# A decoder step on one core: the index projection merged into one product of 584 columns, x transposed through a scaled identity, and the small tables loaded as rows

## The chip, the cores and the metric

The kernel runs on one core of a Trainium2 chip. The metric is the device time of one execution in microseconds (us); the time of a kernel is the median of its runs. All data are float32 unless a line says otherwise.

## What is computed

One inference step of a one-layer decoder for a prompt of 512 tokens and eight samples of eight tokens (64 rows), 576 tokens of width 1024 in all. The part that the change touches:

```
def project_mixer_inputs(xn, w_in, pos):            # xn = rms_norm(x, attn_norm_g)
    q, k, v, qi, ki, wi, u, ga, gb = jnp.split(xn @ w_in, cuts, axis=-1)
    q = rope(...); k = rope(...); qi = rope(...)     # qi: 8 index heads of 64
    ki = rope(ki)                                    # one index key of 64 per token
def indexer_select(qi, wi, ki_all, q_pos, n_sel):    # wi: 8 weights per token
    s = einsum('bqhd,bld->bqhl', qi, ki_all) * IDX_DIM ** -0.5
    score = einsum('bqhl,bqh->bql', relu(s), wi * N_IDX_HEADS ** -0.5)
    _, idx = lax.top_k(where(admissible, score, -inf), n_sel)
```

After it come attention over the selected keys (the samples read keys, values and index keys from a paged cache through `page_table`), a pooling branch, two gates, an output product with a residual, a mixture of 32 experts with two chosen per token, and a last norm. The columns of `w_in` for qi, ki and wi lie side by side: 512, 64 and 8 of them, from column 1024.

## The kernel before

It is written engine by engine, each with its own order of instructions, tied together by semaphores. There is no scheduler: the order in the text is the order on the engine. Tokens go in five tiles (`TILES`): four of 128 prompt tokens and one of 64 sample rows. Everything lives in one SBUF tensor `arena`, cut up by hand, and in the eight banks of `psum`.

The front of the program, around which the change is made, runs so:

- **Loads.** SyncE's queue issues the identity and a column `lane` (L418), the five tiles of x (L420), the page table as eight broadcast loads of single columns (L424), the two norm gains and the pooling scale, turned on the way so that each partition gets single elements (L425 to L427), the 72 columns for ki and wi (`kiww`, L428), the 512 columns for qi (ring slot 0, L442), the rest of the constants with the rotary tables (L445), the history and the pooling weights (L446, L447), the columns for q (L442). L452 then writes zeros into 8 MB of `y_d`, once GpSimd has cleared `zrow`. A "ring" of two slots holds the blocks of 512 columns, and `load_ring(n)` waits until the products of block n-2 are done (`RING_USED`).
- **Norm and transposition.** For each tile ScalarE sums the squares (L1085), takes the root (L1088) and later writes x times 1/rms into `xs` (`scale_x`, L1076), after VectorE's reciprocal (L1340). TensorE transposes `xs` in eight blocks (L613), VectorE multiplies by the gain on the way out of PSUM into `xnT` (L1354). VectorE waits for all three gain loads (`gain_in`, 48) in front of its first L1354, and its third reciprocal stands behind that wait.
- **First products.** `first_product(i)` makes ki and wi of tile i (72 columns, L590), and ScalarE takes them (L1096, L1097). Then come the qi products of tiles 1 to 4 (`QI_ORDER`, 512 columns, L590); tile 0 needs none, since its tokens see fewer keys than are selected. GpSimd gathers the index keys of the samples from the cache (L1662), then rotates ki of each tile (`rotate`, L1693 to L1704) and stores it (L1716), and rotates the jobs of the list `JOBS` (qi, q, k), each after ScalarE's copy out of PSUM (`take_raw`, L1113).
- **Index scores.** `turn_keys` (L633 to L639) and `turn` (L625) transpose the rotated keys and queries, `turned` (L1067) copies them out. `index_prompt(j)` multiplies them (L652), ScalarE applies relu (L1134) and VectorE adds up the eight heads with their weights (L1367 for the first, L1370 for seven more), for j = 0, 1, 2 over 256, 384 and 512 keys. TensorE makes the product of tile i+2 or of q between them.
- **Selection.** VectorE then makes the weights of the samples (L1372) and selects, by rounds of eight (L1383, L1385), for three prompt tiles and for the samples; the last mask is written at L1406. Beside it TensorE scores the samples (L676 to L698), then makes q, k, u (L590, L587), the pooling branch (L728 to L740) and six parts of the gates (L756). Attention starts with L772, and its second unit needs VectorE (L1436) behind the masks.

## Time and profile before

| | us |
|---|---|
| median of 3 runs | 1123.46 |
| lowest and highest | 1121.77, 1126.6 |
| the profiled execution | 1127.28 |
| its span | 1125.7 |
| TensorE busy | 945.2 (84%) |
| VectorE busy | 337.1 (30%) |
| ScalarE, GpSimd busy | 207.3, 201.1 (18% each) |

Time inside the profile counts from the start of the span. Matmuls appear as PE, weight loads as PEld. A float32 product of one block shows as two MATMUL instructions, a transposition as one. "SPq" is SyncE's queue, and an issue there is not the transfer: the transfer lands later.

### The profile page before, as it was taken

Reading aid. Unit: us, or ns where it says so; the run is one execution under the profiler, and the core shown is the slowest. Engines: PE = TensorE matmul, PEld = TensorE weight load, DVE = VectorE, ACT = ScalarE, POOL = GpSimd, SP = SyncE. Lnnn points to the kernel's source line nnn. Section 1 sums busy time; section 2 is a strip of 40 time slices with the busy share of each in tenths; the row PEclk is TensorE's granted clock in tenths of the full one; section 3 lists DMA queues with packets and bytes.
Section 4 is the critical chain, followed back from the end, with each engine's and each line's share of the span. In section 5 each row is a group of like instructions: output and inputs, shape, how many; then the busy total and the mean of one; then the engine's idle time right before and its main releaser. Section 6 shows DMA issues by size and latency. Waiting matters only on the chain.

```text
span 1125.7 us, 11532 instructions
## 1 busy us (share of the span) xinstructions
PE 945.2 (84%) x4386; PEld 506.7 (45%) x4386; DVE 337.1 (30%) x736; ACT 207.3 (18%) x450; POOL 201.1 (18%) x312
## 2 busy tenths in 40 slices
PE   3997999989999998989994998878778887878860
PEld 3643444667776656764552433333233332332320
DVE  1059999993341110331225001000000000000006
ACT  4144111212334334000221100000000000000012
POOL 2750452100001110000132111111111111011113
PEclk9998999999999999999996999999999999998995
DMA  6950022332202645943025999999999999999947
GB/s 210 391 195 1 5 99 91 109 122 75 76 1 75 223 152 159 334 158 150 19 92 213 387 406 425 426 423 424 423 423 424 426 424 423 424 424 425 416 165 245
DMA packets 56414, 283.72 MB, mean 252 GB/s; under 512 B 13224, under 2 KB 13944, under 8 KB 37423
## 3 DMA queue, kind: packets, MB, share of 16 engines
q1 hardware_dynamic: 45591, 246.23, 54.7%
q0 software_dynamic: 10784, 36.97, 9.0%
q8 instruction: 25, 0.41, 0.1%
q14 instruction: 14, 0.11, 0.0%
HBM read 267.38 MB, written 23.17 MB: 258 GB/s over the span
## 4 chain that ended last, share of the span: by engine, by line
PE 64%; DVE 18%; issue 7%; ACT 4%; DMA 4%; SPq 3%; POOL 0%; POOLq 0%; ACTq 0%; DVEq 0%
PE psum L994 21%; PE psum L1009 10%; PE psum L756 8%; DVE arena L1385 6%; DVE arena L1383 6%; PE psum L910 5%; PE psum L590 4%; PE psum L892 3%; DMA arena<-in_w_branch_pool 2%; PE psum L1002 1%; PE psum L844 1%; DVE arena L1611 1%; ACT arena L1283 1%; ACT arena L1287 1%; PE psum L810 1%
## 5 line engine op out<-in xcount | busy, mean ns | idle before, releaser
L994 PE MATMUL psum<-arena 128*64 128x512 f32 x992 | 236.9, 632 | 55.9 <-issue 55.1
L994 PEld LDWEIGHTS psum<-arena 128*64 128x64 f32 x992 | 85.8, 145 | 205.5 <-issue 205.5
L1009 PE MATMUL psum<-arena 128*64 128x512 f32 x512 | 116.9, 597 | 17.7 <-ACT arena L1287 17.7
L756 PE MATMUL psum<-arena 128*128 128x288 f32 x480 | 126.0, 415 | 0.0
L590 PE MATMUL psum<-arena 128*128 128x512 f32 (+2 forms) x320 | 120.2, 535 | 2.1 <-ACT arena L1152 2.1
L756 PEld LDWEIGHTS psum<-arena 128*128 128x128 f32 x480 | 89.6, 192 | 30.9 <-issue 8.1
L1611 DVE TENSOR_TENSOR arena<-arena,psum 128x256 f32<-128x256 f32 x32 | 13.5, 421 | 289.6 <-ACT arena L1283 289.6
L1283 ACT ACTIVATE arena<-psum 128x256 f32<-128x256 f32 x32 | 12.3, 383 | 415.8 <-PE psum L994 405.0
L590 PEld LDWEIGHTS psum<-arena 128*128 128x128 f32 (+1 forms) x320 | 57.6, 207 | 55.0 <-issue 52.4
L1009 PEld LDWEIGHTS psum<-arena 128*64 128x64 f32 x512 | 40.5, 136 | 72.1 <-issue 72.1
L892 PE MATMUL psum<-arena 128*128 128x288 f32 x256 | 64.3, 415 | 5.9 <-DMA arena<-in_w_branch_pool 5.9
L1615 DVE COPY arena<-psum 128x512 f32<-128x512 f32 x32 | 22.1, 691 | 157.1 <-PE psum L1009 157.1
L1383 DVE MAX8 arena<-arena 64x8 f32<-64x1032 f32 (+3 forms) x80 | 66.2, 828 | 2.8
L1797 POOL CAST arena<-arena 128x1 int32 x30 | 5.5, 183 | 329.1 <-DVE arena L1615 329.1
L1385 DVE MATCH_REPLACE8 arena<-arena 64x1032 f32<-64x1032 f32 (+3 forms) x76 | 61.8, 814 | 0.0
L1067 ACT COPY arena<-psum 128x512 f32<-128x512 f32 (+6 forms) x104 | 46.9, 495 | 67.3 <-PE psum L783 32.0
L892 PEld LDWEIGHTS psum<-arena 128*128 128x128 f32 x256 | 49.6, 194 | 20.6 <-DMA arena<-in_w_branch_pool 6.8
L910 PE MATMUL psum<-arena 128*128 128x512 f32 x128 | 55.8, 593 | 1.1 <-issue 1.1
L1665 POOL DMA_INDIRECT arena<-xn_d,arena x32 | 33.4, 1043 | 34.2 <-POOL arena L1791 25.9
L1669 POOL DMA_INDIRECT y_d<-arena x32 | 33.1, 1034 | 29.0 <-POOL arena L1797 27.4
L910 PEld LDWEIGHTS psum<-arena 128*128 128x128 f32 x128 | 23.9, 190 | 29.7 <-issue 29.7
L1773 POOL TENSOR_TENSOR arena<-arena 128x1024 f32<-128x1024 f32 (+1 forms) x5 | 11.7, 2350 | 141.2 <-ACT arena L1271 141.2
(249 smaller groups left out, 882.8 us busy)
## 6 DMA issues: line engine op xcount, KB each, us to landing
arena<-in_w_exp_down SPq DMA_DIRECT2D x32, 2048.0 KB, 22.9
arena<-in_w_exp_gate SPq DMA_DIRECT2D x31, 2048.0 KB, 17.8
arena<-in_w_exp_up SPq DMA_DIRECT2D x30, 2048.0 KB, 22.3
arena<-in_w_in SPq DMA_DIRECT2D x8, 2048.0 KB, 8.7
y_d<-arena SPq DMA_DIRECT2D x1, 8192.0 KB
arena<-in_x_prompt SPq DMA_DIRECT2D x8, 512.0 KB, 7.5
arena<-in_w_out SPq DMA_DIRECT2D x2, 2048.0 KB, 10.7
arena<-in_w_exp_up SPq DMA_DIRECT2D x4, 1024.0 KB, 12.9
```

The costliest lines, as they stand in the source:

```text
L590: last = pe.matmul(bank(b, n, slice(0, r)), lhs, w[:, k, 0:n], start=(k == 0), stop=(k == KD - 1))
L756: last = pe.matmul(bank(2 + n % 2 if n < SAMPLE_G else 2, HN), ring[slot % 2][:, k, m * P:(m + 1) * P], xnT[:, k, HN * hh:HN * hh + HN], s ...
L892: last = pe.matmul(bank(b, HN), w[:, 4 * br + k, m * P:(m + 1) * P], src[:, k, tc], start=(k == 0), stop=(k == 3))
L910: last = pe.matmul(bank(4 + 2 * (i % 2) + half), sgA[k][:, i * P:(i + 1) * P], ring[half][:, k, :], start=(k == 0), stop=(k == KD - 1))
L994: last = pe.matmul(bank(2 + s, 512, rows).rearrange("p (w n) -> p w n", w=2), x_k, wgu[s][:, :, DE * k + 256 * q:DE * k + 256 * q + 256], ...
L1009: last = pe.matmul(bank(4 + s, 512, slice(64 * half, 64 * half + 64)), hT[s][:, k % 2, CAP * (k // 2):CAP * (k // 2) + CAP], wd[s][:, k, 5 ...
L1067: last = act.copy(out, src(b))
L1383: link(dve.max(m8, src))
L1385: link(dve.match_replace(w, m8, src, LOW))
L1611: dve.tensor_tensor(hb[s], sg[s], bank(2 + s, DE // 2, at0=DE // 2), ALU.mult).then_inc(m["h_ready"], 1)
L1665: pool.indirect_dma_start(xg[s], None, xn2_d, bass.IndirectOffsetOnAxis(ap=sidx[s], axis=0), bounds_check=2 * NT - 1, oob_is_err=False).th ...
L1669: pool.indirect_dma_start(y_halves, bass.IndirectOffsetOnAxis(ap=syid[s], axis=0), yo[s], None, bounds_check=2 * FIRST - 1, oob_is_err=Fal ...
```

## The change

Five things are edited together.

1. **One product.** The 584 columns of qi, ki and wi are loaded as one block `wqi` (a place of its own, in front of the ring), and `qi_product` makes them for tiles 1 to 4 in two halves of 292 columns. Tile 0 gets ki alone, 64 columns. The 72-column block, `first_product` and the first ring load are gone, and the ring starts with q.
2. **x through a scaled identity.** ScalarE no longer scales x. VectorE multiplies the identity by 1/rms (`scaled_ident`, 128 by 128), and TensorE multiplies x by that in place of the transposition (`turn_x`). All four prompt tiles are turned first; the sample tile follows after the product of tile 1.
3. **Small loads as rows.** The gains come as 20 rows of 128 and the page table as 8 rows of 8, issued from ScalarE's queue, and TensorE transposes them. VectorE widens the page table in between.
4. **GpSimd's order.** The gathers go in two fours in front of jobs 0 and 1, the key of a tile is rotated with its query as a ninth head, and the keys are transposed in parts (0 and 1, 2, 3, then the samples).
5. **Constants and zeros.** The rotary tables are loaded ahead of the rest, `zrow` moves to the end of the arena, and nothing holds back its clearing. ScalarE's wait for `fill_out` in the pooling branch is gone.

TensorE, from the start to the first index scores. L613 are transpositions of x, L590 products; in the changed kernel L616 turns x, L628 is the key of tile 0 and L604 the product in halves. Before:

```order
L613 MATMUL psum<-arena 128x128 x16
L590 MATMUL psum<-arena 128x72 x8
L613 MATMUL psum<-arena 128x128 x8
L590 MATMUL psum<-arena 128x72 x8
...
L590 MATMUL psum<-arena 64x72 x8
L590 MATMUL psum<-arena 128x512 x14
L633 MATMUL psum<-arena 128x128 x4
...
L590 MATMUL psum<-arena 128x512 x8
L625 MATMUL psum<-arena 128x128 x4
L590 MATMUL psum<-arena 128x512 x2
L652 MATMUL psum<-arena 128x256 x8
```

The same place in the changed kernel (L621 and L623 transpose the gains and the page table, L649 keys, L641 the query, L663 are the scores):

```order
L621 MATMUL psum<-arena 128x20
L623 MATMUL psum<-arena 128x8
L616 MATMUL psum<-arena 128x128 x32
L628 MATMUL psum<-arena 128x64 x8
L604 MATMUL psum<-arena 128x292 x16
L616 MATMUL psum<-arena 128x64 x8
L604 MATMUL psum<-arena 128x292 x32
L649 MATMUL psum<-arena 128x128 x2
L641 MATMUL psum<-arena 128x128 x4
L663 MATMUL psum<-arena 128x256 x8
L604 MATMUL psum<-arena 64x292 x16
```

The four full-width products, which stood between the transpositions and the first scores as 24 blocks of 512, are three products of 16 halves now, and the product of the sample tile has moved behind the first scores.

GpSimd, from its first row of work to its second index query. L1662 and L1698 are the gathers, L1704 and L1737 the sums of a key, L1716 and L1742 its store. Before:

```order
L1662 DMA arena<-in_cache_idx_k,arena 128x512 x8
L1675 MEMSET arena 128x512
...
L1704 TENSOR_TENSOR arena<-arena 64x64 x2
L1716 DMA out<-arena 64x64
L1693 TENSOR_TENSOR arena<-arena 128x8x32 x2
```

And in the changed kernel:

```order
L1708 MEMSET arena 128x512
...
L1742 DMA out<-arena 128x64
L1698 DMA arena<-in_cache_idx_k,arena 128x512 x4
L1726 TENSOR_TENSOR arena<-arena 128x9x32 x2
L1727 TENSOR_TENSOR arena<-arena 128x9x32
L1728 TENSOR_TENSOR arena<-arena 128x9x32
L1737 TENSOR_TENSOR arena<-arena 128x64 x2
L1779 TENSOR_TENSOR arena<-arena 128x512
L1742 DMA out<-arena 128x64
L1698 DMA arena<-in_cache_idx_k,arena 128x512 x4
```

The clearing of `zrow` now comes first, and eight gathers and five keys no longer stand ahead of the queries: four gathers and one key do.

The diff, cut to what the sections above name:

```diff
-        RING_LOADS = [w_in_v[:, :, c:c + 512] for c in (C_QI, C_Q, C_K, C_U)]
+        RING_LOADS = [w_in_v[:, :, c:c + 512] for c in (C_Q, C_K, C_U)]
-        RING_USED = [(S["jp"], v) for v in (9, 14, 19, 24)] + [(S["g_done"], v) for v in (8, 16, 24, 32, 48, 64)]
+        RING_USED = [(S["jp"], v) for v in (10, 15, 20)] + [(S["g_done"], v) for v in (8, 16, 24, 32, 48, 64)]
...
-                for j in range(NPAGE):
-                    src = page_table[:, j:j + 1].rearrange("b j -> j b").to_broadcast([GR, DB])
-                    sp.dma_start(pgi[GR * j:GR * (j + 1), :], src).then_inc(S["page_in"], 16)
-                sp.dma_start(gain1, attn_norm_g[0].rearrange("(k p) -> p k", p=P)).then_inc(S["gain_in"], 16)
...
-                sp.dma_start(kiww, w_in_v[:, :, C_KI:C_KI + KIW]).then_inc(S["kiww_in"], 16)
+            sp.dma_start(wqi, w_in_v[:, :, C_QI:C_QI + QIW]).then_inc(S["wqi_in"], 16)
+            c1 = where["bandcur"][0]
+            sp.dma_start(arena[:, c0:c1], consts[:, c0:c1]).then_inc(S["tab_in"], 16)
...
+            def qi_product(i):
+                r = rows_of(i)
+                pe.wait_ge(S["xn_ready"], 2 * (i + 1))
+                b = QI_BANK[i]
+                for k in range(KD):
+                    lhs = xnT[:, k, i * P:i * P + r]
+                    for half in range(2):
+                        out = bank(b, QIH, slice(64 * half, 64 * half + 64)) if r == 64 else bank(b + half, QIH)
+                        last = pe.matmul(out, lhs, wqi[:, k, QIH * half:QIH * half + QIH], start=(k == 0), stop=(k == KD - 1))
+                last.then_inc(S["jp"], 1)
+
+            def turn_x(i):
...
+                pe.wait_ge(S["dg_ready"], i + 1)
...
-                        last = pe.transpose(bank(g % 2, r, at0=k * P), xs[i % 2][0:r, kk * P:(kk + 1) * P], ident[0:r, 0:r])
+                        last = pe.matmul(bank(g % 2, r, at0=k * P), xin[i][0:r, kk * P:(kk + 1) * P], diag[i % 2][0:r, 0:r], start=True, stop=True)
...
+            pe.wait_ge(S["gain_in"], 48)
+            pe.transpose(bank(2, 20), grow, ident[0:20, 0:20]).then_inc(S["gain_t"], 1)
+            pe.wait_ge(S["pg_wide"], 1)
+            pe.transpose(bank(3, DB), pgw, ident[0:DB, 0:DB]).then_inc(S["gain_t"], 1)
+            for i in range(PT_TILES):
+                turn_x(i)
+            pe.wait_ge(S["wqi_in"], 16)
+            for k in range(KD):
+                last = pe.matmul(bank(6, HD), xnT[:, k, 0:P], wqi[:, k, NI * HD:NI * HD + HD], start=(k == 0), stop=(k == KD - 1))
+            last.then_inc(S["jp"], 1)
+            qi_product(1)
+            turn_x(PT_TILES)
+            pe.wait_ge(S["je"], 1)
+            qi_product(2)
...
+            pe.wait_ge(S["je"], 2)
+            pe.wait_ge(S["xn_ready"], 2 * TILES)
+            qi_product(3)
+            turn_keys(0, 1)
+            turn(0, 4, P, P)
+            index_prompt(0)
+            pe.wait_ge(S["je"], 4)
+            qi_product(PT_TILES)
+            turn_keys(2)
+            turn(1, 4, P, P)
+            index_prompt(1)
+            ring_ready(R_Q)
+            project(0, ring[R_Q % 2], 512)
+            turn_keys(3)
+            turn(2, 4, P, P)
+            index_prompt(2)
...
-                act.activation(xs[i % 2][0:r, :], xin[i][0:r, :], ACT.Copy, scale=rstd1[0:r, i:i + 1]).then_inc(S["xs_ready"], 1)
+            for row, g in ((0, attn_norm_g), (8, ffn_norm_g), (16, pool_scale)):
+                n = g.shape[1] // P
+                act.dma_start(grow[row:row + n, :], g[0].rearrange("(k p) -> k p", p=P)).then_inc(S["gain_in"], 16)
+            act.dma_start(pgi, page_table).then_inc(S["page_in"], 16)
...
+            def take_qi(job):
...
+                act.copy(raw[job % 2][0:r, 0:QIH], lo)
+                act.copy(raw[job % 2][0:r, QIH:NI * HD + HD], hi[:, 0:QIH - NI])
+                act.activation(wiS[0:r, i, :], hi[:, QIH - NI:QIH], ACT.Copy, scale=float(HD ** -0.5 * NI ** -0.5)).then_inc(S["je"], 1)
...
+            def scaled_ident(i):
                 dve.wait_ge(S["rt_done"], i + 1)
-                dve.reciprocal(rstd1[:, i:i + 1], rt1[:, i:i + 1]).then_inc(S["rstd_ready"], 1)
-
-            inverse_rms(0)
-            inverse_rms(1)
-            dve.wait_ge(S["gain_in"], 48)
+                link(dve.reciprocal(rstd1[:, i:i + 1], rt1[:, i:i + 1]))
+                if i >= 2:
+                    dve.wait_ge(S["xt_done"], 2 * (i - 1))
+                dve.tensor_scalar(diag[i % 2], ident, rstd1[:, i:i + 1], None, ALU.mult).then_inc(S["dg_ready"], 1)
...
-            pool.wait_ge(S["gi_ready"], 1)
-            for b in range(DB):
-                gather(idxk[:, b, :], i_groups, gidx[:, b:b + 1], s_idx)
...
+                if kind == "qi" and job < 2:
+                    for b in range(4 * job, 4 * job + 4):
+                        gather(idxk[:, b, :], i_groups, gidx[:, b:b + 1], s_idx)
```

## Rows read from the trace of the kernel before

**Rows 1.** Chain of waits, 0 to 60 us: start, us, what.
```profile
11.66 7.57 DMA arena<-in_ffn_norm_g
...
35.07 15.29 PE psum L590 x60
...
58.12 0.44 PE psum L625 x4
```

**Rows 2.** Timeline, VectorE's index scores: start, busy us, engine, line, operation.
```profile
61.59 0.79 DVE L1367 TENSOR_SCALAR arena<-arena 128x256 f32<-128x256 f32 x1 [25.66 <-ACT arena L1134]
...
68.88 0.58 DVE L1367 TENSOR_SCALAR arena<-arena 128x384 f32<-128x384 f32 x1 [1.16 <-ACT arena L1134]
...
80.18 0.66 DVE L1367 TENSOR_SCALAR arena<-arena 128x512 f32<-128x512 f32 x1 [3.63 <-ACT arena L1134]
...
87.91 0.41 DVE L1372 TENSOR_TENSOR arena<-arena,psum 128x256 f32<-128x256 f32 x1
```

**Rows 3.** Timeline, where sample scoring starts and where TensorE waits for the masks.
```profile
88.42 1.94 PE L676 MATMUL psum<-arena 128*128 128x128 f32 x8 [2.19 <-issue]
...
111.52 8.83 PE L590 MATMUL psum<-arena 128*128 128x512 f32 x16 [2.10 <-ACT arena L1152]
...
244.24 4.15 PE L756 MATMUL psum<-arena 128*128 128x288 f32 x16
251.26 0.52 PE L772 MATMUL psum<-arena 64*128 64x128 f32 x4 [2.88 <-DVE arena L1436]
```

**Rows 4.** Timeline: page table issues, a gather, GpSimd's first query, copy of a turned query.
```profile
3.93 4.55 SPq L424 DMA_DIRECT2D arena<-in_page_table  x8
...
23.74 0.95 POOL L1662 DMA_INDIRECT arena<-in_cache_idx_k,arena  x1 [0.30 <-issue]
...
45.91 1.24 POOL L1693 TENSOR_TENSOR arena<-arena 128x256 f32<-128x256 f32 x2 [0.22 <-ACT arena L1113]
...
58.60 0.58 ACT L1067 COPY arena<-psum 128x512 f32<-128x512 f32 x1 [5.00 <-PE psum L625]
```

**Rows 5.** Timeline, tile 0 of x from its landing to TensorE.
```profile
5.37 1.03 ACT L1085 ACTIVATE psum<-arena 128x1024 f32<-128x1024 f32 x1 [2.89 <-DMA arena<-in_x_prompt]
...
6.55 0.29 ACT L1088 ACTIVATE arena<-arena 128x1 f32<-128x1 f32 x1
...
9.40 1.94 PE L613 MATMUL psum<-arena 128*128 128x128 f32 x8 [9.40 <-ACT arena L1076]
```

**Rows 6.** Windows: length, PE, PEld, DVE, ACT, POOL busy (count), PEclk, DMA share, GB/s.
```profile
28.00:29.00 1.00, 1.00 (x7) 1.00 (x6) 0.00 (x0) 0.53 (x3) 0.70 (x2) 1.00 0.97 407
...
36.00:38.00 2.00, 2.00 (x25) 1.93 (x24) 0.00 (x0) 0.29 (x2) 1.60 (x8) 1.00 1.12 387
...
94.00:96.00 2.00, 2.00 (x8) 1.09 (x7) 1.86 (x8) 1.38 (x3) 0.00 (x0) 0.85 0.00 0
...
113.00:115.00 2.00, 2.00 (x4) 0.67 (x3) 1.90 (x5) 0.00 (x0) 0.00 (x0) 0.50 0.00 0
```

**Rows 7.** Timeline, unit prices at the full clock: transpositions, products of 128, 288 and 2 by 256.
```profile
97.82 1.09 PE L676 MATMUL psum<-arena 128*128 128x128 f32 x8
...
205.71 0.39 PE L728 MATMUL psum<-arena 128*128 128x128 f32 x2
...
205.93 0.39 PE L729 MATMUL psum<-arena 128*128 128x128 f32 x2
...
220.39 23.50 PE L756 MATMUL psum<-arena 128*128 128x288 f32 x96
...
201.11 3.67 PE L587 MATMUL psum<-arena 128*64 128x256 f32 x32
```

**Rows 8.** DMA issues by line: KB each and median us from issue to landing.
```profile
arena<-in_w_in SPq DMA_DIRECT2D x8, 2048.0 KB, 8.7
...
arena<-in_page_table SPq DMA_DIRECT2D x8, 0.5 KB, 7.8
...
arena<-in_consts SPq DMA_DIRECT2D x1, 64.5 KB, 1.8
```

More of the change, by code:

```diff
@@ L50 @@
 KIW = HD + NI
+QIW = NI * HD + KIW
+QIH = QIW // 2
 HN = NT // 2
@@ L186, in program @@
         poT = at(POT, 4, NT)
-        zrow = at(POT, 512)
+        zrow = at(AW - 512, 512)
+        wqi = at(ATT, KD, QIW)
         ring = [at(RING + s * SLOT, KD, 512) for s in range(2)]
         stats = at(XNT - 64, 64)
+        grow = at(SMALL, P, rows=20)
         gain1 = stats[:, 0:8]
@@ L463, in _ @@
                 sp.dma_start(vnew[:, b, :], vnat[b * DS:(b + 1) * DS, PT_TILES, :]).then_inc(S["vnew_in"], 16)
-            for n in range(5, 8):
+            for n in range(4, 7):
                 load_ring(n)
@@ L909, in out_proj @@
                     for k in range(KD):
-                        last = pe.matmul(bank(4 + 2 * (i % 2) + half), sgA[k][:, i * P:(i + 1) * P], ring[half][:, k, :],
+                        last = pe.matmul(bank(4 + 2 * (i % 2) + half), sgA[k][:, i * P:(i + 1) * P], ring[(R_OUT + half) % 2][:, k, :],
                                          start=(k == 0), stop=(k == KD - 1))
@@ L1347, in _ @@
                 r = rows_of(i)
-                if half == 0 and i + 2 < TILES:
-                    inverse_rms(i + 2)
-                if g == 2:
-                    dve.wait_ge(S["page_in"], 16 * NPAGE)
-                    dve.tensor_scalar(gidx, pgi, float(GR), const("lane"), ALU.mult, ALU.add).then_inc(S["gi_ready"], 1)
                 dve.wait_ge(S["xt_done"], g + 1)
@@ L1355, in _ @@
                                   gain1[:, 4 * half:4 * half + 4].unsqueeze(2).to_broadcast([P, 4, r]), ALU.mult).then_inc(S["xn_ready"], 1)
+                if half and i + 2 < TILES:
+                    scaled_ident(i + 2)
             dve.wait_ge(S["const2_in"], 16)
@@ L1695, in rotate @@
                 link(pool.tensor_tensor(b[:, :, 1, :], x[:, :, 0, :], t("sin"), ALU.mult))
-                if outs is None:
-                    for h4 in range(2):
-                        four = slice(4 * HD * h4, 4 * HD * (h4 + 1))
-                        last = pool.tensor_tensor(roped[job % 2][:, four].rearrange("p (j g c) -> p g j c", j=2, g=2),
-                                                  rtmp[0][:, four].rearrange("p (g j c) -> p g j c", j=2, g=2),
-                                                  rtmp[1][:, four].rearrange("p (g j c) -> p g j c", j=2, g=2), ALU.add)
-                    return last
@@ new lines, in key_out, with store_key @@
+            def key_out(i, h):
+                r = rows_of(i)
+                c = slice(h * HD, h * HD + HD)
+                for d in range(2):
+                    last = pool.tensor_tensor(kir[0:r, i, HD * d:HD * d + HD], rtmp[0][0:r, c], rtmp[1][0:r, c], ALU.add)
+                last.then_inc(S["ki_roped"], 1)
+            def store_key(i):
+                pool.wait_ge(S["ki_roped"], i + 1)
+                pool.dma_start(ni_rows[i], kir[0:rows_of(i), i, 0:HD]).then_inc(S["ki_out"], 16)
```

194 lines of the change are left out of this document (94 added, 100 removed).

## The prediction

> **What bounds the kernel now.** I read the chain of waits first, for what the end hangs on. From the start it runs over SyncE's small loads: the last gain lands at 19.2 us, and VectorE, which waits for it in front of its first evacuation, lets go of everything behind [rows 1]. In the timeline tile 0 of x is in at 5.4 us and its root is done at 6.8, so some 11 us go by with the data there [rows 5]. Then the chain is TensorE without a break (transpositions, products of 72 and 512 columns) until the first index query is turned at 58.6 [rows 1]. VectorE's scores start at 61.6, 68.9 and 80.2, each pass after a wait for ScalarE and so for TensorE, and end with the weights of the samples at 88.3 [rows 2]. From there VectorE selects without a gap until 250.6. Beside it TensorE starts to score the samples when those weights are there (88.4), starts the q products at 111.5 and is through at 248.4. It then waits 2.9 us for the masks [rows 3]. So both long strands hang on one point, the end of the index scores, and they are nearly equal: what comes off the front moves both, and neither has to be shortened. What follows (attention, gates, experts) starts by semaphores of this chain and has no fixed hour. The zeros for y_d, the one big transfer with an hour of its own, are issued at 31.6 today, and earlier after the change.
>
> I forecast where the three passes start and compare the last one with 80.2.
>
> **The start.** The eight page table issues alone hold SyncE's queue for 4.6 us, and each lands 7.8 us after its issue [rows 4, 8]. They and the three gains leave this queue. As rows they have no price in this trace. Bounds: the identity, 64 KB, landed in 1.8 us, and the element-wise loads in 7.8 [rows 8]. I take 2.5, near the identity, because the new form also moves whole rows; issued from ScalarE by about 2.6 us they are in at about 5. The two little transpositions, VectorE's copy between them and the page index are then done at about 7, beside the root of tile 0, which is ready at 6.84 [rows 5]. Reciprocal and scaled identity (two short VectorE steps with handoffs, 0.8 us in all): TensorE starts at 7.6. ScalarE, without scale_x, needs some 1.4 us a tile and stays ahead. A page of the Trainium skill speaks against an early landing: "DMA: Bandwidth & Descriptors", § Issuing engines are not separate DMA queues, says that transfers of all issuing engines share the same 16 engines and interleave, so a second queue saves issue time only. By that the rows might trail the x tiles; the late-landing rival below has that price.
>
> **Turning x.** A block is a product now, two instructions for one. At the full clock a transposition of 128 takes 1.09 / 8 = 0.136 us. L728 and L729 start 0.22 apart with two instructions each, 0.112 per instruction [rows 7]. So a tile costs 16 x 0.112 = 1.8 us against 1.1. TensorE begins slow, though. Between 28 and 29 it makes 7 instructions in 1 us, though the clock column reads 1.00 there, and between 36 and 38 it makes 25 in 2 [rows 6]: until 33 to 34 it ran at the lower of its two levels, 1.2 GHz, and tile 0's eight transpositions took 1.94 us [rows 5]. When will it rise? Work that began at 111.5 was at 2.4 GHz (0.98) from about 115; work from 88.4 with a gap in it, from about 94.7 (0.85 over 94 to 96); dense work from 20.2 only from 33.5 [rows 3, 6]. So 3.5, 6.3 and 13.4 us after the start. I take 5, between the first two, because the new stream has 128 columns in every instruction, where that of 20 to 33 had 72 in most. Four tiles are 64 x 0.107 = 6.8 us at speed, plus 2.5 for five slow us: all turned at 16.9.
>
> **Waiting for the weights.** wqi is 2.39 MB and queues behind x, which is through at about 9. Loads of 2 MB land in 8.7 us [rows 8]; at the 390 GB/s or so of the full windows it needs 6.1 us and a latency, hence 16 to 17. It just hides; up to 1.5 us late is inside my range. Its copy of constants (0.25 MB) follows and GpSimd needs that at 19.
>
> **The products.** 288 columns take 23.5 / 96 = 0.245 us an instruction [rows 7], so 292 take 0.248 and a tile of 32 takes 7.9 us. The key of tile 0 is 16 weight-bound instructions, 1.8 us (to 18.7). Tile 1 is done at 26.6, the sample tile of x (16 instructions, where eight transpositions were) at 28.3, tile 2 at 36.2, tile 3 at 44.1. Before, the second query's turn ended at 58.6 and TensorE had by then made most of the same columns; the gain up to here is the idle time, the slow clock and the sample product that moved back.
>
> **First pass.** After the turn at 58.6 the first score came at 61.6 [rows 1, 2], of which 0.9 us was a leftover of the next product: 2.1. Now ScalarE stands on this path with its copy of tile 3 (three pieces, 1.1 us) and one of the keys (0.4) ahead of the 0.6 of the query [rows 4]: 44.1 + 3.6 = 47.7. Before, 61.6. Gain here 13.9.
>
> **Second pass.** The sample product now stands behind the first scores. TensorE leaves those at about 49; the product costs 3.67 x 292 / 256 = 4.2 us [rows 7]; turns 0.7; ScalarE's take 1.1, key copy 0.2, query 0.6, and 1.8 to the first relu: 56.9. VectorE is free at 53.8 (61.6 to 67.7 is its pass, 6.1) and waits 3 us. Gain 12.
>
> **Third pass.** Index products 3.4 from 55.1, tile 0 of q 7.0 (16 x 0.43 and a start), ScalarE 0.8 + 0.3 + 0.6, then 2.2 to VectorE: 69.2, where 80.2 stood. **Gain 11.0.** The extra copies and the moved product give back 3 of 14. The pass of 7.7 and the sample weights stay, so selection starts at 77 and the masks end at 239.6.
>
> **GpSimd** must keep up. Zeros and qs first, from 1 us on, nothing waits. Key 0 rotated at 21, four gathers of 1.25, job 0 from 28 to 33, a store, four gathers until 38.7, job 1 until 43.5 (needed at 53), job 2 from 45.5 to 50.2 (needed by ScalarE's next take at 53), job 3 until 61 (needed at 71). A ninth head adds 1/8 to four steps and two small ones, 0.9 us a job, hidden by TensorE's products; without that cover it would cost 0.9 at one pass. The gathers land by 50 and are needed at 77. The ring is ahead: q and k lie ready, u loads at the same point relative to its use. The zeros to y_d run until about 52 with nobody waiting. ScalarE's wait for fill_out was long met, worth nothing. I cost these at nothing.
>
> **Sum.** 11.0 off. The profiled execution took 1127.28 (span 1125.7), 0.34% over the median 1123.46; it would take 1116.3, and the median becomes **1112.5**. Own range: clock rise 3.5 to 6.3 after the start (0.7 less or more), weights up to 1.5 late, 1 us either way in ScalarE's handoffs, 2 for the scatter of runs: 1109 to 1116.
>
> **Rivals.**
> - *The clock rises late*, 13.4 us after the start as from 20.2 on [rows 6], at 21. Then 8.4 more us pass at half speed, 4.2 lost, 1116.7; in the worst such case at 33.5 as now, 10.5 lost, 1123. For it: the one precedent of the front. Against: narrower instructions there. Chance 0.14.
> - *The rows land late*, 7.8 after issue as the old small loads [rows 8], behind x: page table at 10.4, TensorE from 12.2, 4.6 lost, 1117.1. Against: the identity's 1.8. Chance 0.08.
> - *The price of turning is far higher.* Were a block four times a transposition, 0.54 us for 0.136 [rows 7], then 24 to 32 blocks of x would add about 10 us in front and 2 for the sample tile: 1124. The skill's page "TensorE: Matmul & The Clock Gate", Terms, calls the transposing mode 4 times faster for FP32; by that this case would follow. L728 shows 0.22 per product, 1.6 times, so 0.03.
> - *No gain*: the front is shorter, but a strand behind it keeps its hour, the samples' gathers or a ring load. 1123.5. Against: each lies 20 us ahead of its use. 0.03.
> - *Slower*: the front never reaches the high clock, since TensorE alternates with VectorE and ScalarE there. Its place is the products of 292 columns. At half speed turning ends at 21.3, the key at 24.9, and three products and a turn take 50.6: 75.5 in place of 44.1, and the last pass comes 35 us late: some 1147. It decides from a rise later than about 35 us (each us at 1.2 GHz costs half of one against my 12.6, and 11 are there to lose). Against: L756, 288 wide, runs at the full clock. Chance 0.04.
> - A gain above 13 (faster rise, quieter VectorE): 0.02.
>
> **Numbers.** Forecast 0.66. What a measurement of this kernel can tell from no change is about 0.5%, 5.6 us, so faster means below 1117.8: 0.66 + 0.02 + 0.10 of the clock's 0.14 + 0.05 of the late rows' 0.08 = 0.83. Same: the rest of these two, the dear turn and no gain, 0.13. Slower 0.04. The range 1108 to 1120 adds to my own the two milder rivals and leaves out some 0.2.
>
> **What would show it.** Right: first turn of x at 7 to 8 us, all prompt tiles turned by 17 with instructions at 0.11 in the second half, the three scoring passes from about 47.7, 57 and 69, selection from 77, TensorE's wait for the masks still about 3 us, and every later stage moved by the same 11. Wrong: PE instructions of x still 0.21 apart at 20; a gap ahead of the key product for wqi_in; GpSimd ending job 1 after 53; or a wait of VectorE ahead of the third pass above 5 us. If the front gains 11 and the end doesn't, the mistake is in my claim that nothing behind has an hour of its own.

## The result, and the profile after

| | before | after |
|---|---|---|
| median of seven runs each, us | 1123.48 | 1115.16 |
| ratio of the runs, 95% interval | | 0.9898 (0.9876 to 0.9919) |
| profiled execution: time, span, us | 1127.28, 1125.7 | 1115.16, 1113.5 |
| third pass of scores starts, us | 80.18 | 69.43 |
| SyncE issues the load of w_branch_attn, us | 435.16 | 423.76 |

The kernel is faster by 1.0%. The medians differ by 8.3 us; the ratio of the runs, 0.9898, stands for 11.5 us, its interval for 9 to 14. A median of 1112.5 (1108 to 1120) was forecast. In the profiled executions the span is 12.2 us shorter, of which 10.75 are there at the third pass and 11.4 at the load of w_branch_attn. That issue hangs on a semaphore of the main strand, and I use it below as a landmark behind the attention's front. One execution each of two experiments below (1646.04 us in e1_rows_only, 2289.39 us in e4_split_512_72) stands far off for a reason not known, and the ratios leave it out.

The chain of waits of the kernel after, 0 to 60 us, where [rows 1] stood (start, us, what):

```profile
2.29 4.52 DMA arena<-in_page_table
...
8.15 9.64 PE psum L616 x64
17.79 1.73 PE psum L628 x16
19.52 7.92 PE psum L604 x32
27.44 1.93 PE psum L616 x16
29.37 15.95 PE psum L604 x64
...
47.67 0.61 ACT arena L1165
```

The 7.57 us of the last gain are gone. The chain begins with the page table, now 64 numbers in rows, and from 8.15 to 45.32 it is TensorE alone: four tiles turned by scaled identities (L616), the key of tile 0 (L628), three query products (L604) with the sample tile's turn between them. VectorE's passes and the sample weights follow, in place of [rows 2] (timeline: start, busy us, engine, line, operation, idle time before):

```profile
48.31 0.71 DVE L1403 TENSOR_SCALAR arena<-arena 128x256 f32<-128x256 f32 x1 [17.68 <-ACT arena L1165]
...
57.16 0.42 DVE L1403 TENSOR_SCALAR arena<-arena 128x384 f32<-128x384 f32 x1 [2.90 <-ACT arena L1165]
...
69.43 0.70 DVE L1403 TENSOR_SCALAR arena<-arena 128x512 f32<-128x512 f32 x1 [5.01 <-ACT arena L1165]
...
76.31 0.41 DVE L1408 TENSOR_TENSOR arena<-arena,psum 128x256 f32<-128x256 f32 x1
```

The transfers of 0 to 40 us: the rate of each us in GB/s, then issues with KB each and median us to landing:

```profile
GB/s 0 3 145 256 352 399 417 422 397 175 231 348 390 399 404 392 383 383 385 385 387 393 467 436 433 433 311 219 257 307 362 380 390 377 391 393 385 402 422 416
...
arena<-in_w_in SPq DMA_DIRECT2D x1, 2336.0 KB, 13.3
...
arena<-in_x_sample SPq DMA_DIRECT2D x1, 256.0 KB, 8.3
```

At 9 to 11 us the rate falls by half, and the sample tile takes 8.3 us. The index columns, issued at 4.16, are in at about 17.5, 0.3 us ahead of their use.

TensorE's wait for the masks, as in [rows 3], kept its length, and the sixteen product instructions behind it took 5.84 us where the same sixteen ahead of it took 4.15. Timeline of TensorE, then windows of the same stretch (length, PE, PEld, DVE, ACT, POOL busy with counts, PEclk, DMA share, GB/s):

```profile
232.93 4.15 PE L780 MATMUL psum<-arena 128*128 128x288 f32 x16
239.82 0.49 PE L796 MATMUL psum<-arena 64*128 64x128 f32 x4 [2.75 <-DVE arena L1472]
240.25 5.84 PE L780 MATMUL psum<-arena 128*128 128x288 f32 x16
```

```profile
240.00:242.00 2.00, 2.00 (x8) 1.46 (x9) 1.57 (x9) 1.76 (x8) 0.00 (x0) 0.60 0.00 0
242.00:244.00 2.00, 2.00 (x6) 1.38 (x6) 0.03 (x1) 0.00 (x0) 0.00 (x0) 0.54 0.00 0
```

The granted clock is 0.60 and 0.54 there, close to the lower level of 1.2 GHz. The kernel before had the same (5.77 us behind 2.88 us idle), so it doesn't enter the comparison; it comes back below.

### The profile page after: what moved, and what is told of

Its sections match the earlier page's. It is cut to its first block, busy times and chain, and to the rows that moved or that the text cites. A ratio compares the mean times of both kernels' runs of the same rounds, so it can differ in the third digit from the quotient of the medians.

```text
span 1113.5 us, 11556 instructions
## 1 busy us (share of the span) xinstructions
PE 944.4 (85%) x4412; PEld 510.2 (46%) x4412; DVE 338.7 (30%) x743; ACT 201.7 (18%) x445; POOL 198.3 (18%) x296
## 4 chain that ended last, share of the span: by engine, by line
PE 64%; DVE 18%; issue 7%; ACT 4%; DMA 3%; SPq 2%; POOL 1%; ACTq 0%; POOLq 0%; DVEq 0%
PE psum L1018 21%; PE psum L1033 11%; PE psum L780 9%; DVE arena L1421 6%; DVE arena L1419 6%; PE psum L934 5%; PE psum L916 3%; PE psum L604 3%; DMA arena<-in_w_branch_pool 2%; PE psum L1026 1%; PE psum L868 1%; DVE arena L1647 1%; ACT arena L1313 1%; ACT arena L1317 1%; PE psum L834 1%
## 5 line engine op out<-in xcount | busy, mean ns | idle before, releaser
L780 PEld LDWEIGHTS psum<-arena 128*128 128x128 f32 x480 | 89.6, 192 | 31.0 <-issue 8.1
L1313 ACT ACTIVATE arena<-psum 128x256 f32<-128x256 f32 x32 | 12.3, 384 | 418.1 <-PE psum L1018 407.3
L590 PE MATMUL psum<-arena 128*128 128x512 f32 x192 | 86.2, 604 | 2.1 <-ACT arena L1184 2.1
L916 PEld LDWEIGHTS psum<-arena 128*128 128x128 f32 x256 | 49.5, 194 | 18.5 <-DMA arena<-in_w_branch_pool 4.6
L590 PEld LDWEIGHTS psum<-arena 128*128 128x128 f32 x192 | 36.3, 193 | 45.1 <-issue 42.8
L934 PE MATMUL psum<-arena 128*128 128x512 f32 x128 | 55.8, 593 | 1.1 <-issue 1.1
L934 PEld LDWEIGHTS psum<-arena 128*128 128x128 f32 x128 | 23.9, 190 | 29.7 <-issue 29.7
L1821 POOL TENSOR_TENSOR arena<-arena 128x1024 f32<-128x1024 f32 (+1 forms) x5 | 11.7, 2344 | 139.0 <-ACT arena L1301 139.0
```

Source lines behind the costliest of these rows:

```text
L590: last = pe.matmul(bank(b, n, slice(0, r)), lhs, w[:, k, 0:n], start=(k == 0), stop=(k == KD - 1))
L780: last = pe.matmul(bank(2 + n % 2 if n < SAMPLE_G else 2, HN), ring[slot % 2][:, k, m * P:(m + 1) * P], xnT[:, k, HN * hh:HN * hh + HN], s ...
L916: last = pe.matmul(bank(b, HN), w[:, 4 * br + k, m * P:(m + 1) * P], src[:, k, tc], start=(k == 0), stop=(k == 3))
L934: last = pe.matmul(bank(4 + 2 * (i % 2) + half), sgA[k][:, i * P:(i + 1) * P], ring[(R_OUT + half) % 2][:, k, :], start=(k == 0), stop=(k ...
```

## The experiments

All kernels are compared by the same marks, each from its one profiled execution. "Key" is the start of tile 0's key product on TensorE, "pass 3" VectorE's first score of the third pass, "idle" TensorE's wait for VectorE in the attention's front and "behind it" the sixteen product instructions after that wait. The last column is span less landmark.

| kernel | key | pass 3 | idle | behind it | landmark | rest |
|---|---|---|---|---|---|---|
| before | | 80.18 | 2.88 | 5.77 | 435.16 | 690.5 |
| after | 17.8 | 69.43 | 2.75 | 5.84 | 423.76 | 689.7 |
| e1_rows_only | | 71.75 | 2.83 | 5.80 | 427.00 | 689.6 |
| e2_old_loads | 27.5 | 79.10 | 2.03 | 4.15 | 431.86 | 690.1 |
| e3_transposes | 17.8 | 68.09 | 1.95 | 4.15 | 421.26 | 691.7 |
| e4_split_512_72 | 18.4 | 72.30 | 1.80 | 4.15 | 424.90 | 689.3 |
| e5_late_turns | 19.0 | 67.89 | 2.68 | 5.84 | 422.76 | 689.7 |
| e7_warm | 19.5 | 71.09 | 2.73 | 5.84 | 425.46 | 689.8 |
| e8_x4_later | 17.8 | 69.48 | 2.83 | 5.83 | 423.73 | 691.4 |
| e9_warm_x4 | 18.3 | 69.97 | 1.35 | 4.15 | 422.13 | 691.3 |
| e6_gathers_first | 23.8 | 79.46 | 2.86 | 5.77 | 433.56 | 689.8 |
| e11_filler | 18.9 | 70.51 | none | 4.15 | 423.44 | 688.6 |
| e12_best | 16.7 | 64.28 | none | 4.15 | 417.89 | 691.7 |
| after_again | 17.8 | 69.55 | 2.78 | 5.84 | 423.80 | 690.6 |

Two readings make the experiments sharper than their times. From key to pass 3 after, e2, e7, e8, e9 and e11 all need 51.6 to 51.7 us: that path hardly scatters, and whatever moves the key moves pass 3 by as much, as long as the clock stays high behind it. And the rest behind the landmark scatters by 3 us for code that is the same everywhere, so single times can't rank variants that are closer.

### The loads alone, on the kernel before

```
-                for j in range(NPAGE):
-                    sp.dma_start(pgi[GR * j:GR * (j + 1), :], src).then_inc(S["page_in"], 16)
-                sp.dma_start(gain1, attn_norm_g[0].rearrange("(k p) -> p k", p=P)).then_inc(S["gain_in"], 16)
...
+                act.dma_start(grow[row:row + n, :], g[0].rearrange("(k p) -> k p", p=P)).then_inc(S["gain_in"], 16)
+            act.dma_start(pgi, page_table).then_inc(S["page_in"], 16)
```

> The kernel before with one part of the change: gains and page table come as rows on ScalarE's queue and are transposed on TensorE; nothing else moves (the 72 columns, the transpositions, the order of GpSimd stay). Theory A (most of the gain is the idle 11 us behind SyncE's small loads): the second tile of x is turned at about 11.8 instead of 20.15, the rest of the front follows at the same pace, VectorE's third pass starts at about 72 (80.2 before), and the kernel is some 8 us faster than before, 3 short of the full change. Theory B (the idle time is filled, but the ring's 2 MB load, the gathers or the slow clock then hold TensorE): the third pass starts at 76 or later, gain 4 us or less.

Measured: 1119.91 us, ratio 0.9952 (0.9927 to 0.9977); pass 3 at 71.75, 8.4 earlier than before of the 10.75 in all. The two small turns and their copies cost nothing that shows. Theory A holds: most of the gain is the loads'. The other 2.3 us are those of the rest of the change taken together, the new products above all: in this kernel the 72 columns of a tile still cost sixteen instructions of their own, 3.3 us from 13.4 on.

### The change without its loads

```
+                    sp.dma_start(pgi[GR * j:GR * (j + 1), :], src).then_inc(S["page_in"], 16)
...
+                sp.dma_start(gain2, ffn_norm_g[0].rearrange("(k p) -> p k", p=P)).then_inc(S["gain_in"], 16)
...
+            dve.wait_ge(S["gain_in"], 48)
```

> The changed kernel with one part undone: the eight page table columns and the three element-wise gain loads are back on SyncE's queue ahead of the 584 columns; all else as changed. Theory A: x can't leave PSUM before the gains land at about 19, so turning ends at about 27 and the third pass starts at about 79 to 80 against 69.4: the whole gain over the kernel before goes (time as before, plus or minus 2 us). Theory B (the other parts of the change carry it): the third pass at 75 or earlier, 5 us or more still gained over before.

Measured: 1124.33 us, ratio 0.9987 (0.9971 to 1.0003): the gain is gone. VectorE's and TensorE's timelines show the old wait back:

```profile
19.30 1.29 DVE L1383 TENSOR_TENSOR arena<-psum,arena 128x512 f32<-128x512 f32 x2 [10.45 <-DMA arena<-in_ffn_norm_g]
```

```profile
7.70 3.75 PE L622 MATMUL psum<-arena 128*128 128x128 f32 x16 [7.70 <-DVE arena L1371]
20.13 7.33 PE L622 MATMUL psum<-arena 128*128 128x128 f32 x48 [8.69 <-DVE arena L1383]
```

Tile 0 is turned, then everything waits for the last gain. The key comes 9.7 us later than after, and pass 3 by the same 9.7. Its landmark is 3.3 us ahead of before, of which 1.6 come from the faster instructions behind the idle time (4.15 for 5.77 us, below) and not from the front. Together with e1: the loads are worth 8.4 us without the rest of the change and 9.7 with it, the rest 1.1 us with the old loads and 2.3 with the new. So the rest gives more once the front no longer waits, by 1.2 us in single profiles.

### Transpositions instead of the scaled identity

```
-                        last = pe.matmul(bank(g % 2, r, at0=k * P), xin[i][0:r, kk * P:(kk + 1) * P], diag[i % 2][0:r, 0:r], start=True, stop=True)
+                        last = pe.transpose(bank(g % 2, r, at0=k * P), xs[i % 2][0:r, kk * P:(kk + 1) * P], ident[0:r, 0:r])
...
+                act.activation(xs[i % 2][0:r, :], xin[i][0:r, :], ACT.Copy, scale=rstd1[0:r, i:i + 1]).then_inc(S["dg_ready"], 1)
```

> The changed kernel with ScalarE's scaling of x and plain transpositions back in place of the scaled identity; rows, the one product and the orders stay. Theory A (products of x raise TensorE's clock early, and ScalarE's scaling was in the way): x is turned by 17 to 19, the key of tile 0 and the first product run at the lower clock (instructions 0.2 us apart or more up to 22 or later), the third pass starts at 73 to 75 against 69.4, 4 to 5 us slower than the changed kernel. Theory B (a transposition costs one instruction and the scaled identity is a wash): third pass within 1.5 us of 69.4.

Beside the lines shown, the edit sends ScalarE's squares to PSUM and makes the key product wait for them. TensorE's timeline:

```profile
9.43 1.97 PE L615 MATMUL psum<-arena 128*128 128x128 f32 x8 [2.03 <-ACT arena L1104]
11.84 1.97 PE L615 MATMUL psum<-arena 128*128 128x128 f32 x8 [0.44 <-ACT arena L1104]
14.25 1.59 PE L615 MATMUL psum<-arena 128*128 128x128 f32 x8 [0.44 <-ACT arena L1104]
16.65 1.09 PE L615 MATMUL psum<-arena 128*128 128x128 f32 x8 [0.81 <-ACT arena L1104]
17.58 1.90 PE L628 MATMUL psum<-arena 128*128 128x64 f32 x16
```

ScalarE paces it at 2.4 us a tile and TensorE waits for it each time, and yet x is turned by 17.74, where the scaled identities end at 17.79. The sample tile, later, costs 0.64 instead of 1.93 us, so pass 3 is 1.3 us earlier. My theory, that the scaled identity carries a part of the gain, falls: by the trace it costs 1.3 us. The clock didn't depend on it either: eight transpositions take 1.97, 1.97, 1.59 and 1.09 us in turn. The page "TensorE: Matmul & The Clock Gate" of the Trainium skill says in Part 4 that the full clock "doesn't engage" for transposing mode; these rows disagree, since 1.09 is what [rows 7] has for eight at the full clock. The times don't confirm the 1.3 and lean the other way: 1118.61 us with ten runs from 1114.68 to 1121.86, ratio 0.9928 (0.9906 to 0.9950), which overlaps that of after (0.9876 to 0.9919); the profiled execution was the fastest of the ten. Whether ScalarE's part costs time elsewhere in the other nine is open.

### Columns cut 512 and 72

```
-                        out = bank(b, QIH, slice(64 * half, 64 * half + 64)) if r == 64 else bank(b + half, QIH)
+                            out, c = ((bank(b, 512), slice(0, 512)), (bank(b + 1, KIW), slice(512, QIW)))[half]
```

> The changed kernel with the product of tiles 1 to 3 cut into 512 and 72 columns instead of 292 and 292 (same columns, same number of instructions). If a block costs the larger of weight load and columns, the 72 columns cost 0.107 instead of 0.06 per instruction: 8.5 us a tile against 7.95, 0.6 a tile, 1.8 in three. Third pass at 71.2 against 69.4, and 1 to 2 us slower. The other theory (the even cut is worth nothing, since ScalarE and the weight loads hide it): third pass unmoved.

Measured: 1117.0 us, ratio 0.9919 (0.9888 to 0.9950). A tile takes 8.7 us instead of 7.9, from key to pass 3 it is 53.9 instead of 51.6 us, and the key started 0.6 later. So the even cut into 292 columns is worth 2.3 us. That is as much as the whole rest of the change gave over e1; by these single profiles its other parts add up to about nothing, since some of them cost (the scaled identity above, the place of the turns below).

### Turns ahead of the last contraction step

```
+                    if late and k == KD - 2:
+                        late()
...
+            qi_product(3, late=lambda: both(0, 0, 1))
```

> The changed kernel with the turns of keys and query put in front of the last two of eight blocks of the product ahead of them (as the kernel before did), and ScalarE copying the turned tiles ahead of its take of the new product. Theory A (the three gaps of TensorE behind the turns, 0.97, 1.06 and 0.79 us in the changed kernel, and ScalarE's take inside them, are on the path): passes start at about 47.0, 55.1 and 66.8 against 48.3, 57.2 and 69.4; some 2.6 us faster than the changed kernel, all of it kept to the end. Theory B (the query or ScalarE isn't ready that early, so the wait moves into the product): third pass at 69 or later.

Measured: 1113.48 us, ratio 0.9886 (0.9846 to 0.9927). From key to pass 3 it is 48.86 us, 2.78 less than after. Of this 1.24 went back here, because the key started later: the 64 turning instructions took 10.39 instead of 9.64 us in this execution, with nothing changed ahead of them, and the page table landed 0.5 later. TensorE:

```profile
30.55 14.03 PE L606 MATMUL psum<-arena 128*128 128x292 f32 x56
44.41 0.38 PE L651 MATMUL psum<-arena 128*128 128x128 f32 x2
44.63 0.60 PE L643 MATMUL psum<-arena 128*128 128x128 f32 x4
45.07 2.13 PE L606 MATMUL psum<-arena 128*128 128x292 f32 x8
```

The query and keys of earlier tiles are turned while four products (eight instructions) are left, so ScalarE's copies lie beside these instead of behind them.

The kernel before had its turns at this place, and it had the sample tile's product where the changed kernel has it: between the first scores and the second. TensorE before (L587 is the sample tile's product, L625 the turn of a query):

```profile
62.73 2.81 PE L587 MATMUL psum<-arena 128*64 128x256 f32 x24
65.47 0.66 PE L625 MATMUL psum<-arena 128*128 128x128 f32 x4
66.06 1.08 PE L587 MATMUL psum<-arena 128*64 128x256 f32 x8
```

So the 24 blocks of 512 ahead of the first scores were three products, not four, and the sample product did not move. The gain shrinks from 13.3 us at the first pass (61.59 to 48.31) to 11.7 and 10.75 at the next two because the turns went behind the products. With late turns the passes lie 7.93 and 11.41 us apart, for 7.29 and 11.30 before and 8.85 and 12.27 after.

### Warming products, and the sample tile later

```
+            for n in range(WARM):
+                pe.matmul(bank(7, P), ident, ident, start=True, stop=True)
...
+            sp.dma_start(xin[PT_TILES][0:NS, :], x_rows[PT_TILES]).then_inc(s_x[PT_TILES], 16)
```

The first two lines are e7's (products of the identity with itself before tile 0, whose results are unused), the last is e8's (the load moved behind the index columns and tables), and e9 has both.

> The changed kernel with ten idle products of the identity on TensorE (into a bank nobody reads), six from the landing of the identity on and four between and behind the two small transpositions. Theory A (two things end at the same time in the changed kernel, the turning of x at 17.8 and the landing of the 584 columns at about 17.5): the clock rises earlier, turning ends at 16 to 16.5, and the key product of tile 0 then waits for the columns until about 17.6; third pass within 0.5 us of 69.4. Theory B (the slow clock alone holds the front): key product at 16.3, third pass at 67.9.

> The changed kernel with the load of the sample tile of x issued behind the 584 columns and the rotary tables. In the changed kernel the rate of the transfers falls to 175 and 231 GB/s between 9 and 11 us, where the 64 rows of the samples land. Theory A: without them the columns land some 1.5 to 2.5 us earlier, but x is turned until 17.8 as now, so nothing moves by more than 0.3. Theory B (the columns alone hold the front): key product at 16, third pass at 67.9.

> Both of the last two edits together. Theory A (two equal locks): only now does the key product start earlier, at 16 to 16.5, and the third pass at about 67.9 against 69.4. Theory B (either alone is the lock): no earlier than the better of the two single edits.

Measured, a single run each: 1116.86, 1116.67 and 1115.0 us. The warm products stand on the path (from VectorE's copy of the page table to tile 0 it is 2.85 us instead of 1.25) and give little: in e7 the 64 instructions took 9.30 instead of 9.64, in e9 8.61 against 9.41 in e8; the key is later in both. So x was never turned before the columns were in, and whether the two would meet as equal locks stays open. In e8 the rate stays at 400 GB/s from 9 to 15 us and halves at 16 to 18 instead, where the sample tile now lands: the dip belongs to that load, 64 rows of 4 KB. The columns are in at 15.8 instead of 17.5, but TensorE turns x until 17.85 and has no use for them yet, so nothing is gained. e9's landmark alone is early, by 1.6 us, and not by the front, where it is 0.5 late. The place is TensorE's wait in the attention (timeline, and window):

```profile
239.88 0.49 PE L804 MATMUL psum<-arena 64*128 64x128 f32 x4 [1.35 <-DVE arena L1480]
240.30 4.15 PE L788 MATMUL psum<-arena 128*128 128x288 f32 x16
```

```profile
240.00:242.00 2.00, 2.00 (x11) 1.56 (x12) 1.54 (x10) 1.72 (x8) 0.00 (x0) 1.00 0.04 8
```

### Filler products against the fall of the clock

```
+                    if u == 0:
+                        for n in range(FILL):
+                            pe.matmul(bank(7, 288), ident, xnT[:, 0, 0:288], start=True, stop=True)
```

> The changed kernel with five products of 288 columns into an unused bank, ahead of TensorE's wait for VectorE at the start of the attention (2.75 us idle, 237.08 to 239.82 us); their results are used nowhere. In the runs so far the sixteen gate products behind that wait took 5.77 to 5.84 us after an idle time of 2.68 to 2.88 us, and 4.15 us after one of 1.35 to 2.03 us. Theory C (the length of that idle time sets the clock behind it, and the difference is kept to the end): the idle time is 1.4 to 1.5 us, the sixteen products take 4.15 us, the landmark comes at 422.1 instead of 423.8, and the time is 1.7 us lower. Rival D (the clock behind the wait follows what the work before it was, or is chance): 5.84 us stays, landmark 423.8.

```profile
238.67 2.59 PE L804 MATMUL psum<-arena 128*128 128x288 f32 x10
241.19 0.49 PE L797 MATMUL psum<-arena 64*128 64x128 f32 x4
241.61 4.15 PE L781 MATMUL psum<-arena 128*128 128x288 f32 x16
```

Five float32 products are ten instructions, so the filler ran 2.59 us, not 1.3, and took up the whole wait, 0.4 us of it too long. The instructions behind it took 4.15 us. But this doesn't test theory C. In this execution TensorE came later to the wait, at 238.84 us for 237.08 after, and VectorE let go of it only 0.95 later. The last step of VectorE that it waits for, after and in e11:

```profile
239.70 0.07 DVE L1472 DVE_READ_ACCUMULATOR2_ANT arena<- 128x1 f32 x1
...
240.65 0.07 DVE L1476 DVE_READ_ACCUMULATOR2_ANT arena<- 128x1 f32 x1
```

Without the filler TensorE would have been idle for about 1.9 us (estimated from these rows), and waits of 1.35 to 2.03 us left 4.15 us behind them with no filler at all (e2, e3, e4, e9). The same sum for e12 gives 2.1. So the filler's cost is shown, 0.4 us, and its benefit is not. The landmark agrees: VectorE is 0.95 later than after, less 1.69 for the fast instructions, plus the overrun makes 0.3 earlier, and 0.32 was measured. On the same chip e11 ran in 1114.06 us, after_again in 1115.87; the intervals of their ratios (0.9864 to 0.9918, 0.9877 to 0.9933) overlap.

What stands is an observation: 5.77 to 5.84 us behind the wait in all eight executions with 2.68 to 2.88 us idle, 4.15 in all four with 1.35 to 2.03. The length of the wait doesn't decide alone, though. Behind the 2.10 us idle in [rows 3] the first sixteen instructions of q took 8.83 us, where the next sixteen of the same size took 7.03, in the kernel before and after.

### The gathers first

```
+            pool.wait_ge(S["gi_ready"], 1)
+            for b in range(DB):
+                gather(idxk[:, b, :], i_groups, gidx[:, b:b + 1], s_idx)
```

> The changed kernel with all eight gathers of cached index keys issued as soon as the page indices are there (about 7.7 us), ahead of every rotation on GpSimd, instead of four behind each of the first two rotations. Theory A (GpSimd has time to spare, and the earlier page indices were worth nothing by themselves): the first rotation still starts when its copy is there (19.9 us), the third pass at 69.4 to 69.8 us, the landmark (issue of w_branch_attn) at 423.8. Rival B (their 2 MB take their share of a transfer rate that is full): the index columns land some 5 us later than 17.5, the key product starts at about 22, the third pass at 73 to 74, the landmark at about 428.

```profile
7.97 9.41 PE L616 MATMUL psum<-arena 128*128 128x128 f32 x64 [0.71 <-DVE arena L1380]
23.78 3.68 PE L628 MATMUL psum<-arena 128*128 128x64 f32 x16 [6.40 <-DMA arena<-in_w_in]
27.25 10.22 PE L604 MATMUL psum<-arena 128*128 128x292 f32 x32
```

```profile
23.00:25.00 2.00, 1.22 (x6) 1.22 (x6) 0.00 (x0) 0.00 (x0) 0.00 (x0) 0.50 1.05 390
...
31.00:33.00 2.00, 2.00 (x8) 1.50 (x8) 0.00 (x0) 0.00 (x0) 0.00 (x0) 0.86 0.92 332
```

Measured: 1125.03 us in a single run; pass 3 at 79.46, later by 10.0 us, nearly the whole gain of the change. Rival B named the mechanism and half its size. The columns landed 19.6 us after their issue instead of 13.3, so TensorE stood for 6.4 us; then the clock was at 0.50, 1.2 GHz, until past 31: the key took 3.68 for 1.73 us and the first tile 10.01 for 7.92, 4.0 more. "DMA: Bandwidth & Descriptors", § Issuing engines are not separate DMA queues, of the Trainium skill has transfers of all issuers interleave on the same 16 engines; this run bears it out. Against issuing them at once, the change's order of gathers is thus worth 10 us (one profile), a part I had costed at nothing.

### All together, and after once more

e12 has the late turns, e8's order of loads, the filler, and:

```
+                        if i >= 2:
+                            last = pe.transpose(bank(g % 2, r, at0=k * P), xs[i % 2][0:r, kk * P:(kk + 1) * P], ident[0:r, 0:r])
```

> Put together from what the runs gave: transpositions of rotated tiles ahead of the last contraction step (2.0 us), x tiles 2 to 4 scaled by ScalarE and transposed instead of multiplied by the scaled identity, the sample tile's load behind the index columns and tables, and the five filler products. Expected if the parts add: the key product starts at 16.6 to 17.0 (the columns land at about 16.6), the third pass at 65 to 66 us (after: 69.4), the landmark at about 418.5, and the time 4.5 to 5.5 us below the changed kernel's. Rival (parts share a cover: GpSimd's rotations, or the columns' landing, end last instead): the third pass at 67 or later, 3 us or less below.

> The changed kernel unaltered, on the same chip as the last runs: 1114 to 1116 us, ratio 0.989 to 0.991, third pass at 69.4, idle time of TensorE before the first sample step of the attention 2.7 to 2.9 us with 5.84 us behind it, or below 2.1 us with 4.15.

```profile
8.39 5.44 PE L624 MATMUL psum<-arena 128*128 128x128 f32 x32 [0.71 <-DVE arena L1402]
13.66 0.62 PE L622 MATMUL psum<-arena 128*128 128x128 f32 x4
14.61 2.09 PE L622 MATMUL psum<-arena 128*128 128x128 f32 x12 [0.33 <-DVE arena L1410]
16.54 1.90 PE L636 MATMUL psum<-arena 128*128 128x64 f32 x16
```

Measured: 1109.52 us (six runs, 1108.75 to 1111.45), ratio 0.9850 (0.9823 to 0.9878); after_again 1115.87 (1114.05 to 1117.91), ratio 0.9905 (0.9877 to 0.9933). On this chip it is 6.3 us faster than the change and 1.5% faster than the kernel before. Pass 3 is at 64.28, 5.15 us ahead of after, and the parts add up: 1.08 by the earlier key (tiles 2 and 3, scaled by ScalarE meanwhile, are turned from 13.7 to 16.7), 1.29 by the sample tile's turn, 2.78 by the late turns. The landmark is 5.87 ahead, 0.7 more than pass 3: the instructions behind TensorE's wait took 4.15 instead of 5.84 us, and VectorE's last mask, at 233.36 for 238.09, had lost 0.4 by then. Whether the filler has a part in this is open, as said above.

## Why the prediction was right, and where it was off

**What the end hangs on** stood: the end of the index scores moves both strands. The gain is 10.75 us at pass 3, 11.6 at the sample weights, 11.4 at the landmark. "No gain" and "slower" have nothing in the trace.

**The start**, 7.6 against 8.15. The rows were priced at 2.5 us; the page table took 4.5 to land among the x tiles, below the 7.8 of the old small loads. That is the term that was too small. It was in at 6.8 instead of 5, and only 0.55 of these 1.8 us shows at tile 0, because the sum waited for the root of tile 0 (6.84) anyway and priced the reciprocal and the scaled identity at 0.8 where they took 0.45.

**Turning x**, 16.9 against 17.79: 9.3 forecast, 9.64 measured. The instructions start 0.21 us apart until 11.7 and 0.11 from there on, which is the rate of the sum (the sample tile took 1.93 us where 1.8 was taken). The faster ones came 3.6 us after the start, inside the 3.5 to 6.3 given; in e5 and e11, with the same work until then, 5.7. The reason given for taking 5 is tested by no run. The clock column reads 1.00 throughout, so only the counts tell; windows after, columns as above:

```profile
10.00:11.00 1.00, 1.00 (x7) 1.00 (x6) 0.69 (x1) 0.50 (x1) 0.00 (x0) 1.00 1.00 231
...
16.00:17.00 1.00, 1.00 (x11) 1.00 (x11) 0.93 (x4) 0.00 (x0) 0.00 (x0) 1.00 1.04 383
```

The 9.64 hide errors that cancel in part, which is luck: the rise came 1.4 us earlier than the 5 taken (0.7 us less), while 0.112 us an instruction instead of the 0.107 of the sum and short waits between the tiles' halves (0.5 us in all) made up for it.

**The price of turning.** A product is 1.6 times a transposition, as the row of L728 had it, and the fourfold price of the Trainium skill's page "TensorE: Matmul & The Clock Gate", Terms, does not show. But the sum priced the turning as it stands in the change and never asked what transpositions at full clock would do in its place; e3's trace gives the answer, 1.3 us less at pass 3, though its ten times don't show it.

**The weights**, "16 to 17, it just hides": in at 17.5, with TensorE there at 17.79. The chain hardly shows it. e6 shows how thin that cover was.

**The products and the first two passes**: 7.92 for 7.9, 45.3 for 44.1 (0.9 of it from the late end of turning x), passes at 48.3 and 57.2 for 47.7 and 56.9. **The third**: 69.4 for 69.2 (its terms add up to 69.4 as they stand). So the 1.2 us by which the last product ended late had shrunk to 0.2, because each hand-over through ScalarE was priced too high (3.0 us from that product to the first score, for 3.6). Gain 10.75 for 11.0.

**What gives back the 3 of 14.** The forecast named extra copies and the moved sample product. That product had not moved; the turns had (e5). The hours came out right all the same, because each pass was added up from the new order of instructions and not from this reason.

**The third pass itself** was taken to last 7.7 us as before. From its first score to the sample weights it took 6.88 for 7.73: VectorE's first four sums of heads took 1.02 us each before, with a wait of 0.52 for ScalarE behind them, and all seven took 0.88 on average after. That gave both strands 0.85 us that the forecast hadn't counted.

**GpSimd** kept up, with job 0's rotation at 28.3, job 1's at 38.7 behind the second four gathers. Its cost of nothing is right for the order in the change, and wrong as a statement on gathers in general.

**The time.** The profiled executions differ by 12.2 us of span, pass 3 by 10.75; of the other 1.45, 0.65 had come by the landmark, from the shorter third pass, and 0.8 lie in the 690 us behind it, which scatter by 3. The median fell by 8.3 in one set of runs and by 12.3 in the last. The 2.7 us between forecast and median is of that size, and no step of the sum answers for it.

## What to carry to other kernels

Ask first what the first instruction waits for: here small loads in element-wise form held a full TensorE back, and turning them into rows gave four fifths of the gain by itself. Before an operation is replaced, try the old one in the new setting: the transpositions' price was taken from a front that ran at the lower clock. Before an experiment is called a test, ask what its profile would have shown without the edit: e11's wait was already short. And put small turns and copies ahead of the last contraction step of a neighbouring product, not behind it.

## What the runs showed of the hardware that was not expected

- TensorE idle for 2.68 to 2.88 us in the attention's front took 1.6 to 1.7 us longer for the next sixteen instructions, in eight executions of eight (granted clock after: 0.60 and 0.54); idle for 1.35 to 2.03 us it did not, in four of four. Elsewhere in the same kernels 2.10 us of idle time were enough (8.83 us for 7.03). How long it idles in the attention's front differs between executions: e9's work ahead of the wait ran at the slow rate for longer and began its 96 gate instructions at 210.53 us, for 209.08 after.
- The front's rise to the faster rate is not fixed: the 64 turning instructions took 9.64, 9.56, 10.39 and 10.39 us in four executions whose work on TensorE was the same until then (after, after_again, e5, e11).
- A load of 256 KB over 64 rows halved the rate of everything, from 400 to some 200 GB/s, for two to three us wherever it was put (9 to 11 us after, 16 to 18 in e8); why is not known.
- Warming products ahead of the work bought 0.3 to 0.8 us and cost 1.6, in a single run each.
